# The mixer's relative bias moved from a matmul into VectorE's row maximum, with a table of 128 skewed rows, and one RNN gate in another PSUM bank

## The chip, the cores and the metric

The kernel runs on one core of one Trainium2 chip. The metric is the device time of one execution, in microseconds. The engines that matter here are TensorE (PE, with its weight loads PEld), VectorE (DVE), ScalarE (ACT), GpSimd (POOL, here only an issuer of DMAs and a few fills) and SyncE (SP, which issues the weight DMAs). They run their own instruction streams in order and wait for each other by semaphores.

## The reference, cut to what matters

Two transformer blocks run on 256 tokens of width 1024. The change lies in the first block's mixer. One projection of width 7424 feeds an eight-head window attention (`swa_attention`), an RG-LRU branch and an eight-head attention over one block of 256 tokens (`moba_attention`). Both attentions add a relative bias that depends only on the distance of query and key:

```
s = einsum(q, k) * (HEAD_DIM ** -0.5)
s = where(valid, s + bias_a[t5_bucket(diff)], NEG_INF)
m = maximum(max(s), sink);  p = exp(s - m)
p = p / (sum(p) + exp(sink - m));  o = einsum(p, v)
```

The second attention does the same without a sink. The RG-LRU branch needs two gates, r and i, each a block-diagonal matmul of the convolved input followed by a sigmoid. All arithmetic is float32.

## The kernel before

A float32 weight slab of 1 MB ([128, 8, 256]) is loaded by SP into one of four raw buffers (`sp_weights`, line 507). ACT rounds it to a high part (`act_hi`, line 1245), DVE subtracts to get the low part (`dve_lo`, line 1825), and PE multiplies with three matmuls per tile (lines 626 to 628). The first use of a raw buffer's contents by the next slab waits until DVE has taken the previous one. Between these slabs come 1 MB slabs of the modulation weights, which DVE itself multiplies (`dve_mslabs`, lines 1849 and 1852).

The mixer is a list of 29 slots `zjob`, one slab each: qa, qa, kv, qc, qc, kc, kc, vc, vc (slots 0 to 8), then xr and yr in turn (slots 9 to 16), then twelve gate slabs (17 to 28). In slot t each engine does its own list, in an order written out by hand:

- PE (`pe_mixer`, `pe_z_side`): the slab's matmuls; the values of head t-9; the transposes of the probabilities of head t-8; the score of head t-6; in slots 11, 13, 15, 17 the two gate matmuls of RNN part j.
- ACT (`act_mixer`): it empties the slab's bank, casts the slab of slot t+3, copies out the values of head t-9 (line 1332) and the transposed probabilities of head t-8 (line 1337), then waits for the maximum of head t-6 and takes its exponentials (line 1343), then the gate work of the RNN (line 1362 and after).
- DVE (`dve_mixer`): normalises the probabilities of head t-7 (line 1966), RNN work, `dve_lo` of slot t+3, the row maximum of head t-6 (line 1950), convolution, then modulation slabs.

The score of a head (`pe_score`) is a [128, 128] and a [128, 256] piece in one PSUM bank, each the sum of two float32 matmuls: query by key (line 749), and the bias. The bias matmul (line 752) multiplies a tile `BI[h % 4]` by the flip matrix `JJ`. Row p of `BI` is a 256-long stretch of the head's 384-long bias row, starting at p; the flip puts the rows in the right order. The 16 bias rows come from one small matmul after slot 1, are copied to SBUF by ACT (`rows`, line 1433), written by POOL to DRAM as (16, 384) (line 556), and read back per head with overlapping rows (line 563). The read for head h goes out when the score of head h-4 is complete.

PSUM banks are handed out in rings: slab results take banks 0 to 2 (`Z_G`), scores take 3 and 4 (`Z_S`), everything else, both RNN gates included, takes 5 to 7 (`Z_T`). `take` makes PE wait until the last user of the bank has been read out. A score bank is released by ACT's second exponential.

Of the kernel before, what the change touches and what calls it, by code (L numbers as in the profile page):

```python
# [8 lines left out]
F = mybir.dt.float32  # L9
# [3 lines left out]
AX = mybir.AxisListType.X  # L13
# [13 lines left out]
CAP = 128  # L27


C_ID, C_BO, C_J, C_ROT = 0, 128, 256, 512  # L30
C_COS, C_SIN, C_FD, C_FL = 640, 896, 1152, 1408
C_OHA, C_OHC, C_TRI, C_IOTA, C_EIDX, C_ONE = 2432, 2816, 3200, 3328, 3456, 3464
C_END = 3592
# [11 lines left out]
def constants():  # L45

    c = np.zeros((128, C_END), np.float32)
    p = np.arange(128)
    c[:, C_ID:C_ID + 128] = np.eye(128)
    c[:, C_BO:C_BO + 128] = (p[:, None] // 64 == p[None, :] // 64)  # L50

    for m in range(128):
        half = (m // 16) % 2
        c[m + 16 if half == 0 else m - 16, C_ROT + m] = -1.0 if half == 0 else 1.0
    tok = np.arange(S, dtype=np.float32)
    row, col = np.floor(tok / 64), np.mod(tok, 64)
    freqs = (np.float32(10000.0) ** (-np.arange(16, dtype=np.float32) / np.float32(16))).astype(np.float32)
    for m in range(128):
        d = m % 64
        ang = (row if d < 32 else col) * freqs[d % 16]  # L60
        c[m, C_COS:C_COS + S] = np.cos(ang.astype(np.float32))
        c[m, C_SIN:C_SIN + S] = np.sin(ang.astype(np.float32))
    w = 2 * np.pi * np.outer(p, p) / 128
    c[:, C_FD:C_FD + 128] = np.cos(w) / math.sqrt(128)
    c[:, C_FD + 128:C_FD + 256] = np.sin(w) / math.sqrt(128)
    for tb in range(2):
        w = 2 * np.pi * np.outer(p + 128 * tb, np.arange(S)) / S
        c[:, C_FL + tb * 512:C_FL + tb * 512 + 256] = np.cos(w) / math.sqrt(S)
        c[:, C_FL + tb * 512 + 256:C_FL + tb * 512 + 512] = -np.sin(w) / math.sqrt(S)
    for t in range(384):  # L70
        diff = 255 - t
        b = t5_bucket(diff)
        c[b, C_OHA + t] = 1.0
        c[b, C_OHC + t] = 1.0
        c[32, C_OHA + t] = 0.0 if 0 <= diff < 128 else NEG
        c[32, C_OHC + t] = 0.0 if diff >= 0 else NEG
    c[:, C_TRI:C_TRI + 128] = (p[:, None] < p[None, :])
    c[:, C_IOTA:C_IOTA + 128] = p[None, :]
    c[:, C_EIDX:C_EIDX + 8] = 8 - np.arange(8)
    c[:, C_ONE:C_ONE + 128] = 1.0  # L80
    c[:, C_J:C_J + 128] = np.eye(128)[::-1]
    return c


# [115 lines left out]
def build(nc, a, out):  # L200
# [5 lines left out]
    with ctx:  # L206
# [14 lines left out]
        whi = [sb(f"whi{i}", [128, 2048], R) for i in range(NP)]  # L221
        wlo = [sb(f"wlo{i}", [128, 2048], R) for i in range(NP)]
        X = sb("X", [128, 8, S])
        cst = sb("cst", [128, 384])
        one = sb("one", [128, 128])
        vt = [sb(f"vt{i}", [128, 128]) for i in range(4)]
        modT = [sb("mod_m", [128, 48]), sb("mod_a0", [128, 48]), sb("mod_c0", [128, 16]), sb("mod_a1", [128, 48])]
# [3 lines left out]
        nA = sb("nA", [128, 64])  # L231
        sqb = [sb(f"sqb{i}", [128, 512]) for i in range(3)]
        rst = [sb(f"rst{i}", [128, 512]) for i in range(2)]
        ident, bones, JJ = cst[:, C_ID:C_ID + 128], cst[:, C_BO:C_BO + 128], cst[:, C_J:C_J + 128]
        base = at[0]

        HH, HL = sb("HH", [128, 8, S], R), sb("HL", [128, 8, S], R)
# [81 lines left out]
        HB = macc[2:4]  # L319

        banks = [ctx.enter_context(nc.psum_tensor(f"bk{i}", [128, 512], F)) for i in range(8)]
        bias_dram = nc.dram_tensor("bias_rows", (16, 384), F, kind="Internal")

        B = Banks(banks, [sem(f"filled{i}") for i in range(8)], [sem(f"drained{i}") for i in range(8)])
        N = Notes()
# [197 lines left out]
        def pool_main():  # L523
# [26 lines left out]
            pool.wait_ge(*pool_step.now())  # L550
            gates(0)
            gates(1)
            arrived, n = landed("brow", 2)
            for k in range(2):
                pool.wait_ge(*(yield from N.of("rows", k)))
                pool.dma_start(bias_dram[8 * k:8 * k + 8, :], rows[k][8 * k:8 * k + 8, :]).then_inc(arrived, 16)
            pool.wait_ge(arrived, n)
            for h in range(16):
                if h >= 4:
                    pool.wait_ge(*(yield from B.full("score", h - 4)))  # L560
                arrived, n = landed(f"bi{h % 4}", 1)
                N.note(("bi", h), (arrived, n))
                pool.dma_start(BI[h % 4][:, :], bass.AP(bias_dram, h * 384, [[1, 128], [1, 256]])).then_inc(arrived, 16)
                if h in (9, 11):
                    j = (h - 5) // 2
                    pool.wait_ge(*(yield from B.full("rg", j - 2, 1)))
                    gates(j)
# [170 lines left out]
        def pe_score(h):  # L738
            q, k, v, och = heads[h]
            u = take(Z_S, "score", h)  # L740
            if h in (0, 8):
                for j in range(2):
                    pe.wait_ge(*(yield from N.of("QA" if h == 0 else "QC", j)))
                pe.wait_ge(*(yield from (N.of("KA") if h == 0 else N.of("KC", 0))))
                if h:
                    pe.wait_ge(*(yield from N.of("KC", 1)))
            for qb, (o0, nk) in enumerate(SPANS):
                o = u.t[:, o0:o0 + nk]
                pe.matmul(o, q[:, qb * 128:qb * 128 + 128], k[:, 0:nk], start=True, stop=False)
                if qb == 0:  # L750
                    pe.wait_ge(*(yield from N.of("bi", h)))
                t = pe.matmul(o, JJ[:, :], BI[h % 4][:, 256 - nk:256], start=False, stop=True)
            t.then_inc(u.fill(), 1)

        def pe_turn_p(h):
# [17 lines left out]
        def pe_z_side(t):  # L773
# [34 lines left out]
            if t >= 11 and t % 2 and t <= 17:  # L808
                j = (t - 11) // 2
                pe.wait_ge(*(yield from N.of("gw", j)))  # L810
                pe.wait_ge(*(yield from N.of("xc", j)))
                for w in range(2):
                    u = take(Z_T, "rg", j, w)
                    for m in range(2):
                        tt = pe.matmul(u.t[:, m * S:(m + 1) * S], GW[j % 2][:, w, m, :], RT[j % 2][0][:, m, :], start=True, stop=True)
                    tt.then_inc(u.fill(), 1)
# [475 lines left out]
        def act_start():  # L1292
            arrived, n = landed("cst", 2)
            N.note(("cst",), (arrived, n))
            act.dma_start(cst[:, :], a["consts"][:, 0:384]).then_inc(arrived, 16)
            act.dma_start(one[:, :], a["consts"][:, C_ONE:C_ONE + 128]).then_inc(arrived, 16)
            act.wait_ge(*(yield from dve_step.of("vn", 0)))
            arrived, n = landed("vec0", len(vpairs[0]))
# [25 lines left out]
        def act_head(h, step):  # L1324

            q, k, v, och = heads[h]
            st8, s = ST8[h % 4], SS[h % 4]
            if step == 2:
                act.wait_ge(*(yield from B.full("o", h)))
                u = B.at["o", h]  # L1330
                r0 = 64 * (h % 2)
                act.copy(O[r0:r0 + 64, och, :], u.t[r0:r0 + 64, 0:S]).then_inc(u.sem, 1)
                N.note(("O", och, h % 2), u.drained())
            if step == 1:
                act.wait_ge(*(yield from B.full("p", h)))
                u = B.at["p", h]
                act.copy(PTB[h % 4][:, :], u.t[:, 0:384]).then_inc(u.sem, 1)
                N.note(("pt", h), u.drained())
            if step == 0:
                act.wait_ge(*(yield from dve_step.of("max", h)))  # L1340
                u = B.at["score", h]
                for qb, (o0, nk) in enumerate(SPANS):
                    t = act.activation(s[:, o0:o0 + nk], u.t[:, o0:o0 + nk], AF.Exp, bias=st8[:, 2 + qb:3 + qb], scale=0.125,
                                       accum_out=st8[:, 4 + qb:5 + qb])
                    if qb == 0:
                        t.then_inc(act_step.mark("exp0", h), 1)
                    else:
                        t.then_inc(u.sem, 1)
                N.note(("exp", h), u.drained())
                if h < 8:  # L1350
                    act.activation(st8[:, 6:8], st8[:, 2:4], AF.Exp, bias=snk[:, h:h + 1]).then_inc(act_step.mark("sink", h), 1)
                    N.note(("exp", h), act_step.now())
# [39 lines left out]
        def act_mixer():  # L1392
            for t, (kind, j, col) in enumerate(zjob):
# [28 lines left out]
                if t == 1:  # L1422
# [7 lines left out]
                    for k in range(2):  # L1430
                        act.wait_ge(*(yield from B.full("rows", k)))
                        u = B.at["rows", k]
                        act.activation(rows[k][:, :], u.t[0:16, 0:384], AF.Copy, scale=8.0).then_inc(u.sem, 1)
                        N.note(("rows", k), u.drained())
                if t and zjob[t - 1][0] in ("qa", "kv", "qc", "kc"):
                    act.wait_ge(*(yield from B.full("norm", t - 1)))
                    yield from act_rstd(("z", t - 1), B.at["norm", t - 1], S if zjob[t - 1][0] == "kv" else 512, 64)
# [503 lines left out]
        def dve_head(h, step):  # L1941
            st8, s = ST8[h % 4], SS[h % 4]
            if step == 0:
# [3 lines left out]
                    dve.tensor_scalar(snk[:, 8:16], snk[:, 0:8], -1.0, None, ALU.mult).then_inc(dve_step.mark("snk"), 1)  # L1947
                u = B.at["score", h]
                for qb, (o0, nk) in enumerate(SPANS):
                    dve.tensor_reduce(st8[:, qb:qb + 1], u.t[:, o0:o0 + nk], AX, ALU.max).then_inc(dve_step.mark("max0", h, qb), 1)  # L1950
                dve.wait_ge(*dve_step.now())
                if h < 8:
                    t = dve.tensor_scalar(st8[:, 2:4], st8[:, 0:2], -0.125, snk[:, 8 + h:9 + h], ALU.mult, ALU.min)
                else:
# [741 lines left out]
```

## Time and profile before

| | us |
|---|---|
| median of 3 runs | 2169.04 (2168.8 to 2170.26) |
| profiled execution, its own time | 2169.39 |
| its span | 2167.8 |
| PE busy | 2074.4 (96%) |
| DVE busy | 1710.9 (79%) |
| ACT busy | 1260.4 (58%) |
| POOL busy | 39.5 (2%) |

The span is the time from the first to the last recorded instruction. The mean granted TensorE clock was 0.974 of full speed. Slots 1 to 28 of the mixer lie between about 58 and 310 us of the span; the scores of the 16 heads lie between 102 and 255 us.

### The profile page before, as it was taken

How to read it: one execution, taken by the hardware profiler on the slowest of the kernel's cores; microseconds unless marked ns; L12 is line 12 of the kernel's file. 1: busy time of each engine (PE TensorE's matmuls, PEld its weight loads, DVE VectorE, ACT ScalarE, POOL GpSimd, SP SyncE). 2: the span in 40 equal slices, each digit the busy share in tenths (PEclk: the TensorE clock that was granted, in tenths of full speed). 3: DMA queues.
4: the chain of work that ended last, by engine and by line, in shares of the span. 5: the costliest groups of instructions: out<-in, count | busy, mean ns of one | idle time of the engine just before them, and what ended most of it. 6: DMA issues, size and time to landing. Idle time of an engine off the chain costs nothing.

```text
span 2167.8 us, 30644 instructions
## 1 busy us (share of the span) xinstructions
PE 2074.4 (96%) x12673; PEld 1846.4 (85%) x12673; DVE 1710.9 (79%) x1845; ACT 1260.4 (58%) x1270; POOL 39.5 (2%) x77
## 2 busy tenths in 40 slices
PE   4999999899999999999999999999999999999997
PEld 4887899899898999999997788887888878888886
DVE  6767697799767776777547888897888978888886
ACT  3457643545334454444346677776777767777775
POOL 3010000000000000000000000000000000000000
PEclk8999999899999999999999999999999999999999
DMA  9853576467764446888536999999999989999994
GB/s 307 269 167 112 167 244 203 147 214 249 238 200 139 156 155 207 296 279 273 185 111 237 329 352 358 353 359 336 351 362 358 364 313 358 357 364 365 363 369 150
DMA packets 332801, 580.71 MB, mean 268 GB/s; under 512 B 10357, under 2 KB 150155, under 8 KB 332656
## 3 DMA queue, kind: packets, MB, share of 16 engines
q1 hardware_dynamic: 329152, 572.57, 75.9%
q0 software_dynamic: 3008, 5.78, 1.2%
q8 instruction: 103, 1.69, 0.3%
q10 hardware_dynamic: 496, 0.33, 0.1%
q14 instruction: 42, 0.34, 0.0%
HBM read 577.56 MB, written 1.07 MB: 267 GB/s over the span
## 4 chain that ended last, share of the span: by engine, by line
PE 83%; DVE 10%; ACT 4%; issue 3%; DMA 0%; SPq 0%; DVEq 0%; ACTq 0%
PE bk L632 14%; PE bk L634 14%; PE bk L633 14%; PE bk L626 9%; PE bk L628 9%; PE bk L627 9%; DVE macc L1852 3%; DVE wlo L1825 2%; ACT whi L1245 2%; PE bk L697 1%; PE bk L1137 1%; PE bk L682 1%; DVE uc L2171 1%; PE bk L683 1%; PE bk L684 1%
## 5 line engine op out<-in xcount | busy, mean ns | idle before, releaser
L1825 DVE TENSOR_TENSOR wlo<-raw,whi 128x2048 fp32r<-128x2048 f32 x475 | 1080.8, 2277 | 281.1 <-ACT whi L1245 280.4
L1245 ACT CAST whi<-raw 128x2048 fp32r<-128x2048 f32 x475 | 902.4, 1901 | 401.2 <-PE bk L634 269.1
L626 PE MATMUL bk<-HH,whi 128*128 128x256 f32 x1480 | 432.8, 292 | 13.2 <-DVE HL L1898 12.6
L627 PE MATMUL bk<-HL,whi 128*128 128x256 f32 x1480 | 423.5, 286 | 0.0
L628 PE MATMUL bk<-HH,wlo 128*128 128x256 f32 x1480 | 423.3, 286 | 0.0
L632 PE MATMUL bk<-whi,xh 128*128 128x512 f32 x896 | 356.1, 397 | 4.9 <-DVE wlo L1825 4.9
L634 PE MATMUL bk<-wlo,xh 128*128 128x512 f32 x896 | 350.6, 391 | 0.0
L633 PE MATMUL bk<-whi,xl 128*128 128x512 f32 x896 | 350.0, 391 | 0.0
L626 PEld LDWEIGHTS bk<-HH,whi 128*128 128x128 f32 x1480 | 289.4, 196 | 19.1 <-issue 16.4
L627 PEld LDWEIGHTS bk<-HL,whi 128*128 128x128 f32 x1480 | 289.3, 195 | 1.4 <-issue 0.7
L628 PEld LDWEIGHTS bk<-HH,wlo 128*128 128x128 f32 x1480 | 288.8, 195 | 0.0
L1852 DVE SCALAR_TENSOR_TENSOR macc<-raw,csil,macc 128x512 f32<-128x512 f32 x280 | 209.9, 751 | 9.3 <-DMA raw<-in_w_mod 0.5
L632 PEld LDWEIGHTS bk<-whi,xh 128*128 128x128 f32 x896 | 169.1, 189 | 39.8 <-DVE wlo L1825 6.6
L634 PEld LDWEIGHTS bk<-wlo,xh 128*128 128x128 f32 x896 | 168.9, 188 | 36.2
L633 PEld LDWEIGHTS bk<-whi,xl 128*128 128x128 f32 x896 | 169.2, 189 | 33.5
L632 PE MATMUL bk<-whi,tth 128*128 128x512 f32 x448 | 177.5, 396 | 1.7 <-DVE ttl L2459 1.7
L634 PE MATMUL bk<-wlo,tth 128*128 128x512 f32 x448 | 177.7, 397 | 0.0
L633 PE MATMUL bk<-whi,ttl 128*128 128x512 f32 x448 | 177.5, 396 | 0.0
L626 PE MATMUL bk<-FH,whi 128*128 128x256 f32 x400 | 114.5, 286 | 0.0
L627 PE MATMUL bk<-FL,whi 128*128 128x256 f32 x400 | 113.2, 283 | 0.0
L628 PE MATMUL bk<-FH,wlo 128*128 128x256 f32 x400 | 113.1, 283 | 0.0
L632 PEld LDWEIGHTS bk<-whi,tth 128*128 128x128 f32 x448 | 84.3, 188 | 22.1 <-DVE ttl L2459 1.9
(364 smaller groups left out, 2571.5 us busy)
## 6 DMA issues: line engine op xcount, KB each, us to landing
raw<-in_moe_w SPq DMA_DIRECT2D x336, 1024.0 KB, 5.9
raw<-in_ada_w SPq DMA_DIRECT2D x48, 1024.0 KB, 5.2
raw<-in_ff_w SPq DMA_DIRECT2D x40, 1024.0 KB, 5.6
raw<-in_w_in SPq DMA_DIRECT2D x29, 1024.0 KB, 5.4
raw<-in_w_mod SPq DMA_DIRECT2D x24, 1024.0 KB, 5.5
raw<-in_w_up SPq DMA_DIRECT2D x22, 1024.0 KB, 5.2
raw<-in_attn_w_qkv SPq DMA_DIRECT2D x12, 1024.0 KB, 5.2
raw<-in_w_branch SPq DMA_DIRECT2D x8, 1024.0 KB, 5.5
```

The source lines that it names most:

```text
L626: pe.matmul(o, sh, mh, start=start, stop=False, skip_group_check=True)
L627: pe.matmul(o, sh, ml, start=False, stop=False, skip_group_check=True)
L628: return pe.matmul(o, sl, mh, start=False, stop=stop, skip_group_check=True)
L632: pe.matmul(o, sh, mh, start=start, stop=False, skip_group_check=True)
L633: pe.matmul(o, sl, mh, start=False, stop=False, skip_group_check=True)
L634: return pe.matmul(o, sh, ml, start=False, stop=stop, skip_group_check=True)
L682: pe.matmul(o, xh[:, k, c], h[:, k, :], start=(k == 0), stop=False)
L683: pe.matmul(o, xl[:, k, c], h[:, k, :], start=False, stop=False)
L684: t = pe.matmul(o, xh[:, k, c], l[:, k, :], start=False, stop=(k == 7))
L1245: act.copy(whi[k][:, :n], raw[q.slot[i]][:, :n]).then_inc(q.hi_done.mark(g), 1)
L1825: dve.tensor_tensor(wlo[k][:, :n], raw[q.slot[i]][:, :n], whi[k][:, :n].bitcast(F), ALU.subtract).then_inc(q.taken.mark(i), 1)
L1852: t = dve.scalar_tensor_tensor(out=acc[:, :], in0=v[:, j, :], scalar=sc, in1=acc[:, :], op0=ALU.mult, op1=ALU.add)
```

## The change

The bias is no longer added by PE. The table in DRAM becomes (16, 128, 385): each head's bias row is written 128 times, in rows of pitch 385, by two DMAs that repeat the source (8 rows of SBUF, each read 128 times, 1536 bytes a time, 1.57 MB per DMA). They are issued by ACT, right after it has copied the rows, where POOL issued two DMAs of 12 KB. A tile of head h is then read from offset 127 with pitch 384, so that its rows are already in the right order. The flip matrix goes, and the load of `cst` shrinks from 384 to 256 columns. On DVE the row maximum becomes one `tensor_tensor_reduce`: it adds score and bias, writes the sum to SBUF (`SS`) and gives the maximum. DVE now waits for the head's bias tile where PE did, and it releases the score bank. ACT's exponentials read the sum in SBUF, in place. POOL waits for DVE's release of the score of head h-4 before it reads the tile of head h. The second gate matmul (w = 1) of each RNN part takes its bank from the score ring `Z_S`.

```diff
-        bias_dram = nc.dram_tensor("bias_rows", (16, 384), F, kind="Internal")
+        bias_dram = nc.dram_tensor("bias_rows", (16, 128, 385), F, kind="Internal")
...
-            arrived, n = landed("brow", 2)
-            for k in range(2):
-                pool.wait_ge(*(yield from N.of("rows", k)))
-                pool.dma_start(bias_dram[8 * k:8 * k + 8, :], rows[k][8 * k:8 * k + 8, :]).then_inc(arrived, 16)
-            pool.wait_ge(arrived, n)
+            pool.wait_ge(*(yield from N.of("brow")))
             for h in range(16):
                 if h >= 4:
-                    pool.wait_ge(*(yield from B.full("score", h - 4)))
+                    yield from B.full("score", h - 4)
+                    pool.wait_ge(*B.at["score", h - 4].drained())
                 arrived, n = landed(f"bi{h % 4}", 1)
                 N.note(("bi", h), (arrived, n))
-                pool.dma_start(BI[h % 4][:, :], bass.AP(bias_dram, h * 384, [[1, 128], [1, 256]])).then_inc(arrived, 16)
+                pool.dma_start(BI[h % 4][:, :], bass.AP(bias_dram, h * 128 * 385 + 127, [[384, 128], [1, 256]])).then_inc(arrived, 16)
...
             for qb, (o0, nk) in enumerate(SPANS):
-                o = u.t[:, o0:o0 + nk]
-                pe.matmul(o, q[:, qb * 128:qb * 128 + 128], k[:, 0:nk], start=True, stop=False)
-                if qb == 0:
-                    pe.wait_ge(*(yield from N.of("bi", h)))
-                t = pe.matmul(o, JJ[:, :], BI[h % 4][:, 256 - nk:256], start=False, stop=True)
+                t = pe.matmul(u.t[:, o0:o0 + nk], q[:, qb * 128:qb * 128 + 128], k[:, 0:nk], start=True, stop=True)
...
-                    u = take(Z_T, "rg", j, w)
+                    u = take((Z_T, Z_S)[w], "rg", j, w)
...
-                    t = act.activation(s[:, o0:o0 + nk], u.t[:, o0:o0 + nk], AF.Exp, bias=st8[:, 2 + qb:3 + qb], scale=0.125,
-                                       accum_out=st8[:, 4 + qb:5 + qb])
+                    act.activation(s[:, o0:o0 + nk], s[:, o0:o0 + nk], AF.Exp, bias=st8[:, 2 + qb:3 + qb], scale=0.125,
+                                   accum_out=st8[:, 4 + qb:5 + qb]).then_inc(act_step.mark("exp", h, qb), 1)
...
+                    arrived, n = landed("brow", 2)
+                    for k in range(2):
+                        act.wait_ge(*N.at["rows", k])
+                        act.dma_start(bias_dram[8 * k:8 * k + 8, :, 0:384], rows[k][8 * k:8 * k + 8, :].rearrange("h (o n) -> h o n", o=1)
+                                      .broadcast_to([8, 128, 384])).then_inc(arrived, 16)
+                    N.note(("brow",), (arrived, n))
...
                 for qb, (o0, nk) in enumerate(SPANS):
-                    dve.tensor_reduce(st8[:, qb:qb + 1], u.t[:, o0:o0 + nk], AX, ALU.max).then_inc(dve_step.mark("max0", h, qb), 1)
+                    if qb == 0:
+                        dve.wait_ge(*(yield from N.of("bi", h)))
+                    t = dve.tensor_tensor_reduce(s[:, o0:o0 + nk], u.t[:, o0:o0 + nk], BI[h % 4][:, 256 - nk:256], 1.0, -3.0e38,
+                                                 ALU.add, ALU.max, st8[:, qb:qb + 1])
```

## Rows read from the trace of the kernel before

**Rows 1.** Windows: stretch in us, then busy us by engine, clock, DMA share, GB/s.
```profile
60.00:80.00 20.00, 18.91 (x134) 17.90 (x134) 13.31 (x16) 7.75 (x15) 3.24 (x6) 0.91 0.79 259
80.00:100.00 20.00, 20.00 (x156) 18.23 (x156) 16.69 (x19) 9.87 (x12) 0.00 (x0) 1.00 0.95 310
```

**Rows 2.** Chain that ended last, 50 to 320 us: start, us, what.
```profile
139.51 0.42 PE bk L752 x2
140.55 0.63 PE bk L752 x2
...
161.96 2.29 DVE wlo L1825
164.25 0.54 DVE st L1950 x2
164.82 0.24 DVE st L1953
165.08 0.92 ACT ss L1343 x4
```

**Rows 3.** ACT in order of time: starts of slots 11 and 19, a later copy.
```profile
146.97 1.02 ACT L1409 ACTIVATE rt<-bk,vt 128x256 f32<-128x256 f32 x2 [2.47 <-PE bk L628]
...
236.96 0.59 ACT L1417 COPY GT<-bk 128x512 f32<-128x512 f32 x1
...
239.51 0.47 ACT L1337 COPY ptb<-bk 128x384 f32<-128x384 f32 x1
```

**Rows 4.** PE in order of time, the values of slots 19 and 20.
```profile
233.11 0.65 PE L770 MATMUL bk<-ptb,VC 128*64 128x256 f32 x2
...
242.22 0.65 PE L770 MATMUL bk<-ptb,VC 128*64 128x256 f32 x2
```

**Rows 5.** Waits, 60 to 300 us: total us, times, longest.
```profile
PEld bk L815 <- ACT O L1332: 5.3, 3, 2.9
PE bk L815 <- ACT O L1332: 4.1, 3, 2.5
```

**Rows 6.** DVE operations by line: count, then ns min/median/max.
```profile
L2082 DVE SCALAR_TENSOR_TENSOR ss<-bk,vt,rst x1: 477/477/477, 83.6 to 83.6; 128x256 f32<-128x256 f32 x1
...
L2514 DVE CUSTOM_DVE_ANT_0 CN<-CN,RK x6: 166/166/168, 1204.1 to 1207.9; 128x8 f32<-128x8 f32 x6
L2514 DVE DVE_READ_ACCUMULATOR2_ANT OV<- x6: 80/81/86, 1204.1 to 1208.0; 128x1 f32 x6
...
L2031 DVE TENSOR_TENSOR_SCAN rt<-rt,rt x8: 665/678/691, 169.0 to 237.1; 128x256 f32<-128x256 f32 x8
```

**Rows 7.** ACT exponentials by form: busy us, mean ns (from PSUM, then from SBUF).
```profile
L1343 ACT ACTIVATE ss<-bk,st 128x256 f32<-128x256 f32 x16 | 7.5, 466 | 0.0
...
L1375 ACT ACTIVATE rt<-rt,clam 128x256 f32<-128x256 f32 x8 | 3.6, 500 | 0.0
```

**Rows 8.** DMA queues and issues: packets, MB, share; then KB each, us to landing.
```profile
q1 hardware_dynamic: 329152, 572.57, 75.9%
...
q10 hardware_dynamic: 496, 0.33, 0.1%
...
bi<-bias_rows POOLq DMA_DIRECT2D x16, 128.0 KB, 3.3
...
bias_rows<-rrow POOLq DMA_DIRECT2D x2, 12.0 KB, 3.4
```

**Rows 9.** In time: row copies, weight issue, its landing, cast, first maximum.
```profile
60.90 0.85 ACT L1433 ACTIVATE rrow<-bk 16x384 f32<-16x384 f32 x2
...
64.85 0.37 SPq L507 DMA_DIRECT2D raw<-in_w_in  x1
...
DMA to landing us min/median/max: 8.5/8.5/8.5
...
79.49 1.90 ACT L1245 CAST whi<-raw 128x2048 fp32r<-128x2048 f32 x1
...
106.10 0.61 DVE L1950 TENSOR_REDUCE st<-bk 128x1 f32<-128x128 f32 x2
```

More of the change, by code:

```diff
@@ L27 @@
 CAP = 128
-C_ID, C_BO, C_J, C_ROT = 0, 128, 256, 512
+C_ID, C_BO, C_ROT = 0, 128, 512
 C_COS, C_SIN, C_FD, C_FL = 640, 896, 1152, 1408
@@ L80, in constants @@
     c[:, C_ONE:C_ONE + 128] = 1.0
-    c[:, C_J:C_J + 128] = np.eye(128)[::-1]
     return c
@@ L223, in build @@
         X = sb("X", [128, 8, S])
-        cst = sb("cst", [128, 384])
+        cst = sb("cst", [128, 256])
         one = sb("one", [128, 128])
@@ L233, in build @@
         rst = [sb(f"rst{i}", [128, 512]) for i in range(2)]
-        ident, bones, JJ = cst[:, C_ID:C_ID + 128], cst[:, C_BO:C_BO + 128], cst[:, C_J:C_J + 128]
+        ident, bones = cst[:, C_ID:C_ID + 128], cst[:, C_BO:C_BO + 128]
         base = at[0]
@@ L1294, in act_start @@
             N.note(("cst",), (arrived, n))
-            act.dma_start(cst[:, :], a["consts"][:, 0:384]).then_inc(arrived, 16)
+            act.dma_start(cst[:, :], a["consts"][:, 0:256]).then_inc(arrived, 16)
             act.dma_start(one[:, :], a["consts"][:, C_ONE:C_ONE + 128]).then_inc(arrived, 16)
@@ L1340, in act_head @@
                 act.wait_ge(*(yield from dve_step.of("max", h)))
-                u = B.at["score", h]
                 for qb, (o0, nk) in enumerate(SPANS):
-                    t = act.activation(s[:, o0:o0 + nk], u.t[:, o0:o0 + nk], AF.Exp, bias=st8[:, 2 + qb:3 + qb], scale=0.125,
-                                       accum_out=st8[:, 4 + qb:5 + qb])
[L1345 to L1349, printed above, removed]
+                    act.activation(s[:, o0:o0 + nk], s[:, o0:o0 + nk], AF.Exp, bias=st8[:, 2 + qb:3 + qb], scale=0.125,
+                                   accum_out=st8[:, 4 + qb:5 + qb]).then_inc(act_step.mark("exp", h, qb), 1)
+                N.note(("exp", h), act_step.now())
                 if h < 8:
@@ L1949, in dve_head @@
                 for qb, (o0, nk) in enumerate(SPANS):
-                    dve.tensor_reduce(st8[:, qb:qb + 1], u.t[:, o0:o0 + nk], AX, ALU.max).then_inc(dve_step.mark("max0", h, qb), 1)
+                    if qb == 0:
+                        dve.wait_ge(*(yield from N.of("bi", h)))
+                    t = dve.tensor_tensor_reduce(s[:, o0:o0 + nk], u.t[:, o0:o0 + nk], BI[h % 4][:, 256 - nk:256], 1.0, -3.0e38,
+                                                 ALU.add, ALU.max, st8[:, qb:qb + 1])
+                    if qb == 0:
+                        t.then_inc(dve_step.mark("max0", h), 1)
+                    else:
+                        t.then_inc(u.sem, 1)
                 dve.wait_ge(*dve_step.now())
+                dve.wait_ge(*u.drained())
                 if h < 8:
```

## The prediction

> **What bounds the kernel now.** I read the windows first, then the chain of waits, then the engines in order of time. PE is busy 96% of the span, so what PE is spared counts wherever PE itself is the last to be waited for. In the mixer this changes with the stretch. From 80 to 100 us PE is full and the DMA engines are 95% busy at 310 GB/s [rows 1]. From 102 to 147 us (slots 6 to 11, heads 0 to 4) the chain runs through PE alone, the bias matmuls included, and ACT waits 2.47 us for PE at the start of slot 11 [rows 2, 3]. From slot 11 to slot 18 the chain leaves PE. It goes round a loop of ACT and DVE: empty the bank, cast a slab, DVE's subtraction 2.29, the row maximum 0.54, the scaling 0.24, the exponentials 0.92, the RNN work, and again [rows 2]. Slot 11 starts on ACT at 146.97 and slot 19 at 236.96, which is 90.0 us for eight slots [rows 3]. PE has idle time here: its waits for the second gate's bank alone add to 9.4 us [rows 5]. From slot 20 on PE paces the chain again, and no later stage is tied to a fixed moment, so what the mixer gains or loses goes through to the end.
>
> **PE's part.** The bias matmuls of one head stand in the chain with 0.42 and 0.63 us [rows 2], 1.05 us together; 16 heads make 16.8 us of PE. Heads 0 to 4 lie before slot 11, where PE is waited for: 5 x 1.05 = 5.25 us. I checked that ACT and DVE keep up there: a slot of their loop costs about 0.5 + 1.8 + 2.3 + 0.9 + 0.24 + 0.92 and the gaps and small exponential, some 7.2 us with the new maximum, against 8.06 for PE's slot (9.11 between the values of slots 19 and 20 [rows 4], less 1.05). The heads of slots 11 to 18 are spared in PE's idle time and bring nothing by themselves.
>
> **DVE's part.** The two reductions take 0.61 us with their overlap [rows 9]. The trace has the new operation only on eight columns, as a custom instruction of 0.166 and an accumulator read of 0.08. An operation of two inputs, one of them in PSUM, takes 0.477 for 256 columns [rows 6]; for 128 I take 0.34 (128 columns less, at the 1.1 ns of DVE's subtraction, 2.29 us for 2048 columns [rows 2]). With two reads of 0.08 and the same overlap this is about 0.9: 0.3 more per head. Lower bound: nothing more, if the read hides. Upper bound: the scan's rate, 0.678 for 256 columns [rows 6], gives 1.2, 0.6 more. I take 0.3, since the eight-column instruction costs no more than a plain one. In slots 11 to 18 it is on the loop: 8 x 0.3 = 2.4 us lost. The exponentials read SBUF instead of PSUM: 500 ns against 466 [rows 7], but the 500 is of another line; I take nothing, at most 0.03 x 16.
>
> **The exit from the loop.** ACT's slot 19 starts at 5.25 - 2.4 = 2.85 us earlier. PE's next step after it, the values of slot 20, started at 242.22, although the probabilities it needs were copied out at 239.51 + 0.47 = 239.98 [rows 3, 4]. PE, spared its matmuls, will be there in time, so this 2.24 goes too: 5.1. The scores of heads 14 and 15 follow with PE as the pace: 2.1. Sum for the arithmetic: 7.2 us less.
>
> **The gate's bank.** Its 9.4 us of PE's waiting [rows 5] lies in the stretch that ACT and DVE pace. Without it PE runs ahead until it meets the same copies by ACT at slots 19 and 20. I cost it at nothing. Cover: the loop. If DVE and ACT were faster there, it would be worth up to 9.4. New waits of the score ring (the score of slot 12 waits for DVE's release of slot 11's) fall behind a whole slab's matmuls, over half of a 9.11 us slot, and cost nothing.
>
> **The table.** This is the step that decides. Each DMA now reads eight SBUF rows 128 times, 8 x 128 x 1536 bytes = 1.57 MB, 3.15 MB in both, in place of 24 KB. ACT issues them at about 61.8 us, behind its row copies [rows 9]; two issues of about 0.4 us are covered, as ACT then waits for slot 2. POOL waits for both, then issues the four tile loads, 3.3 us to landing [rows 8], which with 0.5 for the issue is 3.9. DVE needs the first tile at its first row maximum, at 106.10 [rows 9]; behind that instruction stand DVE's slab work and ACT's exponentials, hence everything. The wait therefore starts to cost when the table takes more than 106.1 - 3.9 - 62.2 = 40 us.
>
> The trace has no transfer of this form. Fast end: the weight queue moves 572.57 MB in 75.9% of 2167.8 us, 348 GB/s [rows 8], so 3.15 MB take 9.0 us. Slow end: all eight rows through one engine's sixteenth, 21.8 GB/s: 144 us. A 1 MB slab fills 128 partitions with 16 engines, which is eight partitions to one engine's rate; the table is read out of eight partitions only. The one old row with that source moves 12 KB in 3.4 us [rows 8], all of it latency, and tells no rate. I take two engines' worth, 43.5 GB/s, near the slow end: 72 us. Then the table lands at 134 + 0.5, the first tile at about 138.5, and DVE waits 32.4 us. The weight slabs that share the engines become slower at the same time, but DVE's wait covers this. Effect: 32.4 - 7.2 = 25.2 us slower.
>
> The Trainium skill says in "SBUF — State Buffer", section "Door 1: The DMA port swizzle", that a transfer touching few partitions is held to the ports that they reach, one port for each four of the low partitions at about 27 GB/s (measured 27.6 GB/s for partitions 0..3). No row here shows that. By it each DMA would use two ports and both would take 58 us, an estimate, the wait would be 18 us and the kernel 11 us slower before any loss of the weight stream. In "DMA: Bandwidth & Descriptors", section "Why a DMA increments its semaphore by 16 and not by 1", it says that the outermost dimension, here 8, limits the number of engines to 8; that alone would be the second rival.
>
> **From the profiled execution to the median.** The sum is made against 2169.39 (span 2167.8 and 1.6 around it), 0.35 above the median of 2169.04. 2169.0 + 25.2 = 2194.2.
>
> **Rivals.**
> 1. The table is written at the full rate, by all engines. Its 9 us start at 62, while the weight queue has some 4 idle us in 60 to 80 (share 0.79 [rows 1]), and the slab issued at 64.85, cast at 79.49 [rows 9], needed 8.5 us to land and can be 6 late. So no delay, and the arithmetic's 7.2 us are the result: 2161.8 (to 2165 with the scan's rate). For it: a broadcast is only a repeated address. Against: eight source rows.
> 2. Eight engines, one source row each at 21.8 GB/s: 0.393 MB per engine, 18 us. The table is there at 85, long before 106, but these engines also carry half of every slab, at a stretch that is 95% busy. If the two queues alternate packet by packet, the table takes 60% of them until about 92. The slab due at 79.49 and those after it come 5 to 8 us late. Result: 7 - 7.2, no change, 2169 (2164 to 2173).
> 3. The table is slow and the weight stream is held by it as well. At two engines' worth over eight engines each table packet of 1536 bytes keeps its engine for 0.28 us; a slab has 64 packets of 1 KB per engine, and with one table packet before each it needs 18 us, where PE takes one per 3.4 us (1 MB at 310 GB/s [rows 1]). In a table's time T some four slabs (14 us of PE's work) land, and 6 us of lead are there: delay T - 20, net T - 27. For T from 50 to 72 us this is 23 to 45 slower, 2202 with T = 60. It is the forecast's mechanism with another wait in front (ACT waits for raw slabs instead of DVE for the tile), decided by whether two queues share an engine evenly while one of them is slow.
> 4. The scan's rate or worse for the new operation, alone: 8 x 0.6 = 4.8 against 9.6 gained; about 2164.5. It only moves rival 1 towards no change.
>
> **How the numbers follow.** A measurement of this kernel tells 0.2%, about 4.3 us, from no change: the bounds are 2164.7 and 2173.4. The slow table, forecast and rival 3 together: 0.60 (0.38 and 0.22). Rival 1: 0.25, of which 0.02 falls within no change by rival 4. Rival 2: 0.13. Something else: 0.02. Faster 0.25, same 0.15, slower 0.60. The forecast's own range is 2178 (a table of 56 us) to 2210. The range for 8 in 10 must take in rival 1, so it is 2161 to 2210; left out are a table slower than 87 us and savings larger than 8.
>
> **What would show it.** Right: DVE's first new maximum starts well after 106 and its idle time ends with the DMA of `bi` from `bias_rows`; the ACT queue's share of the engines rises from 0.1% [rows 8] to above 1%; the mixer's loop in slots 12 to 18 is 0.3 us longer per slot; PE has no wait for ACT before the gates; the scores take 1.04 us. Wrong: if the first maximum is on time (105 to 107) and ACT's cast never waits for a raw slab, the table was fast and rival 1 holds. If ACT or DVE wait for raw slabs between 70 and 110 us, it is rival 2 or 3. If the gate's bank mattered, slots 12 to 18 would be shorter on ACT, not longer.

## The result and the profile after

The changed kernel takes 2199.61 us, median of four runs (2197.05 to 2202.75), against 2169.65 for the kernel before in the same comparison. The ratio is 1.0139, 95% interval 1.0127 to 1.0151: 30 us slower. The forecast was 2194, slower, with a range of 2161 to 2210, so time, sign and range held. The wait that costs the time is not the one the forecast named: it is the one of rival 3.

The first view is the windows of the kernel after, in the stretch that [rows 1] show for the kernel before (the same columns).

```profile
60.00:80.00 20.00, 12.85 (x80) 11.53 (x80) 6.37 (x9) 4.89 (x11) 0.00 (x0) 0.81 0.70 173
80.00:100.00 20.00, 14.77 (x107) 13.89 (x105) 7.68 (x9) 3.87 (x5) 0.00 (x0) 0.93 0.69 150
100.00:120.00 20.00, 9.36 (x58) 8.00 (x58) 5.77 (x7) 1.82 (x4) 0.00 (x0) 0.76 0.69 138
120.00:140.00 20.00, 13.17 (x73) 11.99 (x74) 11.54 (x13) 8.50 (x10) 2.33 (x4) 0.65 0.83 267
```

PE, full at 80 to 100 us before, is busy 9.4 of 20 us at 100 to 120. All compute engines lose busy time together, and the bytes moved fall from 310 to 138 GB/s although the DMA engines are still 69% busy. Busy engines that move little: that is the mark of slow packets.

The second view is the waits of the kernel after, 55 to 340 us (total us, times, longest).

```profile
POOL bi L559 <- DMA bias_rows<-rrow: 109.4, 1, 109.4
...
ACT whi L1237 <- DMA raw<-in_w_in: 39.4, 4, 21.9
...
ACT rst L1264 <- issue: 15.1, 1, 15.1
...
PE bk L762 <- ACT ptb L1329: 8.7, 4, 3.6
...
DVE macc L1845 <- DMA raw<-in_w_mod: 3.9, 1, 3.9
```

ACT waits 39.4 us for raw weight slabs. There is no row of DVE waiting for a bias tile. In order of time (start us, us):

```profile
61.60 15.37 ACTq L1425 DMA_DIRECT2D bias_rows<-rrow  x2
...
98.65 1.90 ACT L1237 CAST whi<-raw 128x2048 fp32r<-128x2048 f32 x1 [11.19 <-DMA raw<-in_w_in]
...
123.76 1.90 ACT L1237 CAST whi<-raw 128x2048 fp32r<-128x2048 f32 x1 [21.91 <-DMA raw<-in_w_in]
...
129.07 2.33 POOL L559 DMA_DIRECT2D bi<-bias_rows  x4 [109.38 <-DMA bias_rows<-rrow]
...
143.51 0.28 DVE L1945 CUSTOM_DVE_ANT_0 ss<-bk,bi 128x128 f32<-128x128 f32 x1
```

The table's queue on the page (columns as in [rows 8]), then the landing time of the slab that SP issued at 65.01, and that of the four tile loads issued from 129.07:

```profile
q10 hardware_dynamic: 2560, 3.41, 1.2%
```
```profile
DMA to landing us min/median/max: 33.6/33.6/33.6
```
```profile
DMA to landing us min/median/max: 6.2/6.4/6.5
```

The table is issued from 61.6 and has landed at 129.07: 67 us, 47 GB/s for 3.15 MB. The tile loads land about 6.4 us after their issue, the first one near 135.5, and the first row maximum comes at 143.51: the tile was there first. The maximum is 37.4 us later than at 106.10 [rows 9]. The slab that landed in 8.5 us [rows 9] now takes 33.6. The span is only 29.7 longer (2197.5 against 2167.8), so 7.7 us of the delay are regained behind head 0.

The chain that ended last says the same: from 84.47 to 123.76 it is one wait for a slab, and again before 139.29 (start, us, what). ACT's second table issue, which held ACT for 14.55 us, stands in it too; e7 and e9 below ask what that costs.

```profile
62.42 14.55 ACTq L1425
...
84.47 39.21 DMA raw<-in_w_in
...
128.01 11.20 DMA raw<-in_w_in
```

### The profile page after: what moved, and what is told of

It is laid out like the page before. It is cut to its first block, busy times and chain, and to the rows that moved or that the text cites. A ratio compares the mean times of both kernels' runs of the same rounds, so it can differ in the third digit from the quotient of the medians.

```text
span 2197.5 us, 30579 instructions
## 1 busy us (share of the span) xinstructions
PE 2069.5 (94%) x12609; PEld 1844.2 (84%) x12609; DVE 1711.7 (78%) x1877; ACT 1260.9 (57%) x1270; POOL 38.6 (2%) x75
## 4 chain that ended last, share of the span: by engine, by line
PE 78%; DVE 11%; ACT 5%; issue 3%; DMA 3%; ACTq 1%; SPq 0%; DVEq 0%
PE bk L628 14%; PE bk L630 14%; PE bk L629 14%; PE bk L622 8%; PE bk L624 8%; PE bk L623 8%; DVE macc L1845 3%; DMA raw<-in_w_in 2%; DVE wlo L1818 2%; ACT whi L1237 2%; PE bk L693 1%; PE bk L1129 1%; DVE uc L2172 1%; PE bk L678 1%; PE bk L1092 1%
```

## The experiments

Two theories stood at the start. A: the table's writes are the whole loss, since they hold DMA engines that the weight slabs need, and all the rest saves about 7 us. B: VectorE's new work loses too. Within A it was open whether the narrow source, the number of engines, the bytes or ACT's hold of 14.5 us counts.

**e1: no table.**

```diff
-bias_dram[8k:8k+8, :, 0:384] <- rows[k][8k:8k+8] repeated 128 times
+bias_dram[8k:8k+8, :] <- rows[k][8k:8k+8]          # (16, 384)
-bass.AP(bias_dram, h * 128 * 385 + 127, [[384, 128], [1, 256]])
+bass.AP(bias_dram, h * 384, [[1, 128], [1, 256]])
```

> The changed kernel, with the bias rows written once (two DMAs of 12 KB, issued by ACT) and the tiles read with pitch 1 from them, so each tile's rows come in the reverse order: the bias of the wrong query is added, all else is computed. Theory A (the 3.15 MB table is the whole loss, the rest saves what the prediction's arithmetic says): about 7.5 us faster than the kernel before, 2162, and no wait of ACT for raw slabs. Rival B (the work moved to VectorE loses as well, the table only part of the 30 us): 2169 or more. First row maximum at 106 in both.

Measured: 2161.87, ratio 0.9966 (0.9952 to 0.9980), 7.4 us faster. Its first maximum is at 105.53 and no engine waits for a raw slab. ACT in order of time (slots 11, 12, 19, 24):

```profile
141.17 1.02 ACT L1396 ACTIVATE rt<-bk,vt 128x256 f32<-128x256 f32 x2 [1.25 <-PE bk L624]
153.93 0.56 ACT L1399 COPY O<-bk 128x512 f32<-128x512 f32 x1
...
232.42 0.59 ACT L1404 COPY GT<-bk 128x512 f32<-128x512 f32 x1
...
269.27 0.60 ACT L1406 ACTIVATE GT<-bk 128x512 f32<-128x512 f32 x1 [4.65 <-PE bk L624]
```

Theory A holds, B falls: the move of the bias to VectorE is a gain by itself. e1 also reads its tiles with the old pitch; e4 below reads them as the changed kernel does and comes out at the same ratio, so the pitch of the tiles makes no difference that can be told.

**e2 and e12: the gate's bank in its old ring** (`take(Z_T, "rg", j, w)` in e1 and in e11 below), **e8: the gate's bank alone, in the kernel before.**

> As e1, but the second RNN gate takes its bank from the side ring, as before the change (same wrong order of the bias rows). Theory A (slots 11 to 18 are paced by ACT and VectorE, the gate's bank is worth nothing): equal to e1 within 1 us. Rival C (PE's 9.4 us of waiting for that bank is on the path): 5 to 9 us slower than e1.

> The kernel before with the second RNN gate's bank in the score ring and nothing else. Theory A: slots 11 to 18 are paced by ACT and VectorE, so 0 to 2 us faster or nothing, 2167 to 2170, though PE's 9.4 us of waits for ACT's copy go. Rival C: 5 to 9 us faster, 2161 to 2165. A loss is possible too: here the score banks are only freed by ACT's exponentials, so PE may wait for them.

> As e11, with the second RNN gate's bank back in the side ring. By the prediction's step (worth nothing, ACT and VectorE pace those slots) equal to e11 within 1 us; e1 and e2 differed by 1.1 us, inside their spread. If the gate's bank is worth something small, this run is 1 to 2 us slower than e11.

Measured: e2 0.9974 (0.9963 to 0.9984) against e1's 0.9966; e12 0.9971 (0.9961 to 0.9981), the same as e11; e8 0.9996 (0.9986 to 1.0005). Three times no difference beyond the noise, which is 2 to 3 us here; the 5 to 9 us of rival C are excluded. And this although PE waits more for that bank in e2 than before the change. Waits of e2, 55 to 340 us:

```profile
PEld bk L807 <- ACT O L1324: 12.4, 4, 5.1
PE bk L807 <- ACT O L1324: 10.8, 3, 4.7
```

The two rows are not to be added. PE and PEld are the two halves of one engine and wait at the same time: in the kernel before, both waits end at 172.56, at 195.22 and at 217.20. So the 9.4 us of [rows 5] are about 5.3 us of idle time, and the 23.2 here about 12.4.

With the bank in the score ring these rows are gone and PE waits for ACT's copy of the probabilities instead. Waits of e1:

```profile
PE bk L762 <- ACT ptb L1329: 8.5, 3, 3.5
```

PE's idle time moved; the runs show no sign that it was on the path.

**e3: the kernel before, with the table written and unread.**

```diff
+big_dram = nc.dram_tensor("big_rows", (16, 128, 385), F)
+act.dma_start(big_dram[8k:8k+8, :, 0:384], rows[k][8k:8k+8] repeated 128 times)   # k = 0, 1
```

> The kernel before, with the change's two table writes added from ACT into a DRAM tensor that nobody reads; the only wait on them is ACT's in slot 9, before the source's place in SBUF is written again. Theory A (the writes take engine time from the weight slabs and block ACT while they are issued): about 37 us slower, 2206, with ACT's waits for raw slabs near 40 us. Rival D (the loss needs VectorE's wait for the first bias tile): within 5 us of the kernel before, 2169 to 2174.

Measured: 2207.73, ratio 1.0171 (1.0154 to 1.0188), 37 us slower; ACT waits 40.2 us for raw slabs, the first row maximum is at 145.13, 39.0 late. Nobody reads this table, so a wait for the tile is not needed for any of the loss (rival D falls). The loss of this one edit less the gain of e1 is the whole change: 37.1 - 7.4 = 29.7 us.

**e4 and e11: the same table, made by a DMA from DRAM to DRAM.**

```diff
+act.dma_start(row_dram[8k:8k+8, :], rows[k][8k:8k+8])                 # 24 KB, once
+act.dma_start(bass.AP(bias_dram, 0, [[385, 128], [128 * 385, 16], [1, 384]]),
+              bass.AP(row_dram, 0, [[0, 128], [384, 16], [1, 384]]))  # after the rstd of slot 1
```

> The changed kernel, computing everything, but the rows go to DRAM once (24 KB), and one DMA from DRAM to DRAM, with the 128 copies outermost, makes the table. Same table bytes, no narrow SBUF source, 16 engines. Theory A (what is slow is the source of eight SBUF rows): the table lands within 15 us of its issue, 2162 to 2166. Rival E (3.15 MB of unaligned 1536-byte writes to DRAM are slow whatever the source): the table still takes over 40 us and the time stays above 2185.

> The kernel of e4 again with more rounds, as the base for e12: 0.25 to 0.35% faster than the kernel before, 2162 to 2164.

Measured: e4 2163.38, ratio 0.9965 (0.9951 to 0.9979), and e11, the same kernel again, 2164.21, ratio 0.9971 (0.9961 to 0.9981). The same bytes landed 23.1 us after the issue. I had expected 15, so this is a miss in size: the queue's own engine time (the row below: 0.6% of the span on 16 engines) is 13 us, and while the table was under way (65.3 to 88.5 us) its queue took 50.7% of the engines' time and the weight slabs 55.4% (packets of the two overlap a little). Rival E falls. Queue of the table DMA on e4's page:

```profile
q10 hardware_dynamic: 2592, 3.43, 0.6%
```

That is half the engine time of the change's 1.2%, for the same bytes. This kernel computes everything and is, by e11, 0.29% faster than the kernel before (6 us), 35 us faster than the changed one.

**e5: the source rows apart.** The eight rows of each DMA in partitions 0, 4, 8 to 28.

```diff
-rows[k][8 * k:8 * k + 8, :]
+rows[k][0:32:4, :]            # rnat is loaded with the heads 4 columns apart
```

> The changed kernel, computing everything, but the eight source rows of each table DMA lie in partitions 0, 4, 8 to 28 instead of 0 to 7 and 8 to 15. Still eight outermost rows, still eight engines, same bytes and issue order. Theory P (four neighbouring partitions share one way out of SBUF; 3.15 MB over two of them at a time took 67 us, 47 GB/s): the table is 3 to 4 times faster, landing about 18 to 25 us after its issue, kernel 2163 to 2175. Rival Q (eight engines are slow at re-reading one row each, wherever it lies): lands again after about 67 us, 2200.

Measured: 2166.86, ratio 1.0000 (0.9990 to 1.0011). On e5's page:

```profile
q10 hardware_dynamic: 2560, 3.41, 0.4%
```

Only the place of the rows in SBUF (and how they get there, before the table is issued) is other than in the changed kernel, and the table takes a third of the engine time. By the table's own stretch, in the rows under e6 below, it is 22.2% of 16 engines for 38 us, or 135 engine-us, and 3.15 MB over them is 23 GB/s per engine; in the changed kernel it is 36.7% for 67 us, or 393 engine-us, and 8.0 GB/s. Rival Q falls, theory P stands. The table landed 33.7 us after its issue (61.0 to 94.7), later than the 25 expected. The slabs beside it on the same engines are not the whole reason, since e10 below needs 21.8 us for the same rows. ACT is still held 6.4 us by its second issue and waits 10.1 us for slabs. Why the median shows no gain is open: the profiled execution was the fastest of ten (2160.41; the others 2164.42 to 2171.41), and its first maximum, at 108.59, is only 2.5 us late, so it does not show where a typical one loses.

**e6: one DMA of sixteen rows.**

```diff
-two DMAs, rows[0][0:8] and rows[1][8:16], each repeated 128 times
+one DMA, rows[1][0:16] repeated 128 times
```

> The changed kernel, computing everything, but both halves of the rows are gathered in one tile of 16 partitions and one DMA with 16 outermost rows writes the table. Theory P: sixteen engines, but four ways out of SBUF instead of two, at 47 GB/s for two: about 33 us for the table; all engines are held, so the weight slabs are late for half as long; 2175 to 2190. Rival Q (the number of engines alone): 33 us as well, so this run tells how the loss goes with the table's time, not P from Q. A rival R (the loss is fixed by the 3.15 MB): 2200.

Measured: 2181.09, ratio 1.0060 (1.0043 to 1.0077). The table lands after 35.4 us. Yet the first maximum is at 123.82, 15 us later than e5's 108.59 although the two tables took about the same time. The DMA queues from 62 us to the table's end or a little after it, of e6 (62 to 96), of e5 (62 to 100) and of the changed kernel (62 to 129), the last with the busy tenths of the DMA engines in 40 slices:

```profile
q10 hardware_dynamic: 2063, 3.15, 76.3%
q1 hardware_dynamic: 2299, 3.00, 24.2%
```
```profile
q1 hardware_dynamic: 6645, 8.76, 68.4%
q10 hardware_dynamic: 2064, 3.15, 22.2%
```
```profile
DMA  9999955555556996995555555798569855555558
q10 hardware_dynamic: 2064, 3.15, 36.7%
q1 hardware_dynamic: 5572, 7.27, 32.0%
```

What the weight stream loses is the engines' time in table packets, 76.3% here against 22.2% in e5, not the table's time to landing: 3.00 MB of weights pass in 34 us, against 8.76 MB in 38.

**e7 and e9: GpSimd issues the table DMAs**, in e7 one right behind the other, in e9 the second after the first has landed.

```diff
-act.dma_start(bias_dram[...], rows[k][...] repeated 128 times)
+pool.dma_start(bias_dram[...], rows[k][...] repeated 128 times)
```

> The changed kernel, computing everything, but GpSimd issues the two table DMAs, in place of ACT. ACT was held 14.5 us by its second issue. Theory A1 (ACT's hold is covered by the raw slabs that are late anyway; the engines are the loss): 2190 to 2202. Rival S (ACT's hold is a loss of its own, on top): 12 to 15 us faster than the changed kernel, 2185 to 2188.

> As e7 (GpSimd issues the table DMAs), but it waits for the first to land before it issues the second. e7 changed two things at once: ACT was no longer held, and the table came in 39.5 us instead of 67. Theory T (the two DMAs of e7 ran side by side out of different SBUF neighbourhoods, and the engines held by slow packets are the loss): the table takes 60 to 80 us again and the kernel 2192 to 2205. Rival S (ACT's hold of 14.5 us was the difference): 2180 to 2186, as e7.

Measured: e7 2181.64, ratio 1.0062 (1.0042 to 1.0082), which is below what theory A1 expected and alone would have spoken for rival S. e9 2202.30, ratio 1.0163 (1.0141 to 1.0185). POOL in order of time, e7, then e9:

```profile
61.28 2.20 POOL L555 DMA_DIRECT2D bias_rows<-rrow  x2 [41.62 <-ACT rrow L1425]
102.21 2.19 POOL L564 DMA_DIRECT2D bi<-bias_rows  x4 [38.73 <-DMA bias_rows<-rrow]
```
```profile
60.69 1.13 POOL L557 DMA_DIRECT2D bias_rows<-rrow  x1 [41.12 <-ACT rrow L1427]
96.15 1.08 POOL L557 DMA_DIRECT2D bias_rows<-rrow  x1 [34.33 <-DMA bias_rows<-rrow]
134.03 2.32 POOL L566 DMA_DIRECT2D bi<-bias_rows  x4 [36.80 <-DMA bias_rows<-rrow]
```

Each DMA alone takes 35 to 38 us; side by side both take 41. In e9 ACT is not held, and the loss is no smaller than in the changed kernel. So rival S falls; e7 gained because both DMAs ran at once. GpSimd's DMAs go through another queue than ACT's (q0 software_dynamic on its pages, where ACT's stand as q10 hardware_dynamic), but that is not e7's gain either, since e9 uses it too. The comparison with the changed kernel is not exact, since e9's table takes 73 us instead of 67. An estimate: e7 loses 13.4 us with 41 us of table and e9 35.3 with 73, and the line through both gives 31 for 67 us, where the changed kernel, with ACT held, loses 30. The hold costs nothing that these runs can tell.

**e10: rows apart and GpSimd's issue** (the edits of e5 and e7 together).

> Everything computed; source rows in partitions 0, 4 to 28 as in e5 and the table DMAs issued by GpSimd as in e7. Expected: table landed within 25 us of its issue, no hold of ACT, no late raw slab beyond a few us; 2160 to 2164, 5 to 8 us faster than the kernel before. If GpSimd's issue of so many packets were slow by itself, it would show as a table of over 30 us.

Measured: 2165.41, ratio 0.9981 (0.9972 to 0.9989), 4 us faster than before. The table is there 21.8 us after its issue; slabs are still late by 10.1 us on ACT and 2.9 on DVE, and the gain is below the 5 to 8 us that were expected. e4 and e11 are the better form.

## Why the prediction was right or wrong

**PE's part, right.** In e1 slot 11 starts on ACT at 141.17 against 146.97 [rows 3]; its first maximum was 0.57 early by the stage ahead, which leaves 5.2 us for heads 0 to 4, where 5.25 stood.

**DVE's part, right in sign, the size too large.** The new operation takes 0.284 and 0.420 us for 128 and 256 columns, with accumulator reads of 0.083. From the first maximum to the scaling it is 0.74 us instead of 0.65: 0.09 more per head, where 0.3 stood. DVE, by form, 140 to 295 us of the kernel after (busy us, mean ns):

```profile
L1945 DVE CUSTOM_DVE_ANT_0 ss<-bk,bi 128x256 f32<-128x256 f32 x16 | 6.7, 420 | 0.0
L1945 DVE CUSTOM_DVE_ANT_0 ss<-bk,bi 128x128 f32<-128x128 f32 x16 | 4.5, 284 | 0.0
```

The 0.477 of another operation had been too high, and the scan's rate is excluded. ACT's exponentials from SBUF are slower, 493 ns against 466 for 256 columns [rows 7] and 402 against 367 for 128, about 0.06 us per head, which the prediction took as nothing. Together slots 12 to 18 take 78.5 us in e1 against 77.4 before (159.56 to 236.96): 0.16 per slot, not 0.3.

**The exit and the sum.** e1 is 4.5 us ahead at slot 19 (232.42 against 236.96) and 6.2 at slot 24 (269.27 against 275.46), 5.6 without the early start; its ratio gives 7.4 (4.3 to 10.4). The 7.2 lies inside, but two of its terms were off in opposite directions. The loop lost 1.3 us over its eight slots, not 2.4. The exit gave 1.7, not the 4.3 counted on, since PE was not there in time. PE in order of time in e1, the values of slots 19 and 20, then the windows from 225 to 235 us of e1 and of the kernel before (columns as in [rows 1]):

```profile
226.03 1.08 PE L762 MATMUL bk<-ptb,VC 128*64 128x256 f32 x2 [3.30 <-ACT ptb L1329]
...
238.12 0.65 PE L762 MATMUL bk<-ptb,VC 128*64 128x256 f32 x2
```
```profile
225.00:235.00 10.00, 8.97 (x35) 7.29 (x36) 6.61 (x15) 7.61 (x13) 0.00 (x0) 0.50 0.34 105
```
```profile
225.00:235.00 10.00, 10.00 (x69) 8.46 (x68) 6.26 (x12) 7.71 (x13) 0.00 (x0) 1.00 0.17 45
```

The copy that slot 20's values need had ended at 235.43, so the gap is 2.69 us where the 2.24 of the kernel before should have gone. PE, spared its bias matmuls, had waited 3.30 us for ACT; after that its granted clock was 0.50 (1.2 GHz), where it was 1.00 (2.4 GHz) in the kernel before. In e2 the clock stayed at 1.00 in this stretch and the gap is still 2.4, so the clock is only part of it: PE is full there (18.00 of 18 us from 222 to 240 in e2).

**The gate's bank, right:** nothing beyond the noise, in three comparisons. The price that it was given if it counted, up to 9.4 us, added the waits of PE and PEld, which are the same 5.3 us.

**The table, right that it decides, wrong in the wait.** Its time was predicted at 72 us and measured at 67. The step that failed is "The weight slabs that share the engines become slower at the same time, but DVE's wait covers this". DVE never waited for the tile; the slabs were later than the tile, and ACT waited for them. That is rival 3, whose delay of T - 20 gives 47 for T = 67, where 37.4 was measured: more slabs passed than the four of its working. Three DMA instructions of 1 MB were issued between 60 and 66, then at 82.27 and 84.47, and all five had landed by 123.8; from 62 to 129 the weight queue moved 7.27 MB. That the result lies near 2194 is partly luck, by two errors of opposite sign: the first tile was there near 135.5 instead of at 138.5, which alone would have made the loss smaller, and the slabs held the first maximum some 8 us beyond it. (The 32.4 also counts the half microsecond of the tile's issue twice; the prediction's own 72 and 40 us give 32.0.) **ACT's two issues** were put at 0.4 us each; the second held ACT 14.55 us. By e9 and the estimate beside it the hold cost nothing that can be told, because the slabs were late anyway, but the cover named for it was too small. In the kernel before ACT waits 8.78 us for slot 2, and its work on slot 1 stands ahead of that wait:

```profile
72.39 0.37 ACT L1398 COPY VA<-bk 128x256 f32<-128x256 f32 x1 [8.78 <-PE bk L684]
```

Why the queue holds the issue was not tried.

**Why the table is slow** is shown by e5: eight neighbouring partitions feed eight engines at 8.0 GB/s each, partitions four apart at 23. The Trainium skill states in "SBUF — State Buffer", section "Door 1: The DMA port swizzle", that four neighbouring low partitions share one port of about 27 GB/s. By that a DMA of this form has two ports and needs 29 us, an estimate; e7, e9 and the change (34 to 40 us per DMA beside weight slabs) are not far above it, and here the partitions are read. The Trainium skill also says, in "DMA: Bandwidth & Descriptors", section "Why a DMA increments its semaphore by 16 and not by 1", that an outermost dimension of 8 picks 8 engines. The DMA share of 5 tenths in most slices of the changed kernel's table agrees, as does e6, where the table of 16 rows takes 76.3% of the engines' time, more than eight of them have.

## What to carry to other kernels

Before a DMA repeats a few SBUF rows many times, ask where its source partitions lie and how many engines it takes: a transfer nobody waits for can cost several times its bytes' worth when its packets are slow (37 us in e3, for bytes that take 9 us at the weight queue's 348 GB/s), since the loads on the same engines wait behind them. Look for engines that are busy while the GB/s fall, and judge by engine time per byte of the queue, not by the transfer's own landing time. Here the way out was to let DRAM be the source of the repetition, which turned a loss of 30 us into a gain of 6.

## What the hardware showed that was not expected

- A second large table DMA held ACT's queue for 14.55 us at its issue, with rows in eight neighbouring partitions, and 6.4 us with the rows apart; GpSimd's issue of the same DMA took 1.1 us.
- The same two DMAs took 67 us together from ACT, as long as one after the other, and 41 us side by side from GpSimd. Why ACT's did not run side by side was not tried.
- A row maximum fused with an addition on VectorE costs 0.420 us for 256 columns from PSUM, where the plain reduction took 0.414. The addition and the write to SBUF are almost free; what is new is the accumulator read of 0.083 behind each, of which 0.09 us per head remain.
